# Differential attention on one core: TensorE's value products placed ahead of the transposes within a step

## What is computed

```python
def attend_block(args):                      # diff_attention, one block of 128 queries
    logits = jnp.einsum('bhmqd,bhmkd->bhmqk', qb, k).astype(jnp.float32)
    logits = logits + jnp.transpose(bias, (2, 0, 1))[None, :, None]
    logits = jnp.where(visible, logits, -jnp.inf)
    p = jax.nn.softmax(logits, axis=-1)
    w = p[:, :, 0] - lam * p[:, :, 1]
    return jnp.einsum('bhqk,bhkv->bhqv', w.astype(v.dtype), v)
...
o = rms_norm(o, out_norm_g) * (1.0 - lam_init)

# memory_cross_attention
logits = jnp.einsum('bqhd,bkhd->bhqk', q, k).astype(jnp.float32)
p = jax.nn.softmax(logits, axis=-1)
o = jnp.einsum('bhqk,bkhd->bqhd', p.astype(v.dtype), v)
```

## Time and profile before

| what | value |
|---|---|
| median of 3 runs | 3560.15 us (3557.86 to 3570.12) |
| the profiled execution | 3560.86 us, its span 3559.1 us |
| TensorE busy | 3274.8 us (92%), granted clock 0.955 in the mean |
| VectorE busy | 2348.2 us (66%) |
| ScalarE busy | 974.5 us (27%) |
| GpSimd busy | 1077.6 us (30%) |
| the stage of the change | 2304.4 to 2393.0 us of the span, about 88 us |

### The profile page before, as it was taken

The page is one execution under the profiler, slowest core; times in us unless marked ns, Lnnn a source line. Parts: engine busy times, 40 slices in busy tenths (PEclk is TensorE's granted clock), DMA queues, the critical chain, the costliest instruction groups (busy, mean ns, idle before and its releaser), DMA issues. The chain is left out here.

```text
span 3559.1 us, 53901 instructions
## 1 busy us (share of the span) xinstructions
PE 3274.8 (92%) x18869; PEld 2888.2 (81%) x18869; DVE 2348.2 (66%) x4071; ACT 974.5 (27%) x1683; POOL 1077.6 (30%) x751
## 2 busy tenths in 40 slices
PE   8769999697999999998999998979998998799989
PEld 6458898475999999998999997747886767578867
DVE  5565565746888988877888887476774324367741
ACT  2222222202333343333333333361210012311200
POOL 4111010341121222213333333304554432045544
PEclk9879999898999999999999999999999998699999
DMA  4000000222778777788999992103332320033323
GB/s 139 32 1 2 1 1 1 73 68 96 240 250 272 248 264 258 246 293 319 359 353 340 348 338 91 51 16 99 99 103 65 92 72 14 15 98 94 97 71 97
DMA packets 214325, 508.78 MB, mean 143 GB/s; under 512 B 18534, under 2 KB 102646, under 8 KB 210588
## 3 DMA queue, kind: packets, MB, share of 16 engines
q1 hardware_dynamic: 155420, 322.15, 27.1%
q0 software_dynamic: 36864, 134.23, 11.5%
q10 hardware_dynamic: 21888, 50.34, 3.7%
HBM read 454.21 MB, written 52.44 MB: 142 GB/s over the span
## 5 line engine op out<-in xcount | busy, mean ns | idle before, releaser
L177 PE MATMUL ev_acc<-ev_w_high,ev_high 128*128 128x384 f32 x1024 | 343.1, 335 | 9.2 <-DVE ev_w_low L2365 9.2
L178 PE MATMUL ev_acc<-ev_w_low,ev_high 128*128 128x384 f32 x1024 | 342.8, 335 | 0.0
L179 PE MATMUL ev_acc<-ev_w_high,ev_low 128*128 128x384 f32 x1024 | 342.8, 335 | 0.0
L177 PE MATMUL up_ps<-ffn_high,up_high 128*128 128x512 f32 x704 | 276.0, 392 | 5.5 <-DVEq L646 5.5
L2315 POOL DMA_INDIRECT ev_rows<-in_v,ev_list x128 | 177.4, 1386 | 333.5 <-DVE ev_row_sum L2370 322.8
L179 PE MATMUL up_ps<-ffn_high,up_low 128*128 128x512 f32 x704 | 275.4, 391 | 0.0
L178 PE MATMUL up_ps<-ffn_low,up_high 128*128 128x512 f32 x704 | 275.1, 391 | 0.0
L177 PE MATMUL eu_ps<-norm_unit_high,eu_high 128*128 128x384 f32 x768 | 265.1, 345 | 0.0
L172 POOL TENSOR_TENSOR up_low<-normed,up_high 128x1024 fp32r<-128x1024 f32 x88 | 211.4, 2403 | 176.7 <-DVE up_high L167 176.7
L179 PE MATMUL eu_ps<-norm_unit_high,eu_low 128*128 128x384 f32 x768 | 257.2, 335 | 0.0
L178 PE MATMUL eu_ps<-norm_unit_low,eu_high 128*128 128x384 f32 x768 | 257.0, 335 | 0.0
(11 more groups left out here) (602 smaller groups left out, 8377.8 us busy)
## 6 DMA issues: line engine op xcount, KB each, us to landing
normed<-in_u SPq DMA_DIRECT2D x128, 512.0 KB, 4.8
mixed<-in_v SPq DMA_DIRECT2D x128, 512.0 KB, 5.4
normed<-in_w_up SPq DMA_DIRECT2D x88, 512.0 KB, 3.5
expert_act<-mixed ACTq DMA_DIRECT2D x128, 192.0 KB, 4.2
expert_gates<-eu_gates ACTq DMA_DIRECT2D x24, 1024.0 KB, 6.9
expert_scores<-expert_gates SPq DMA_DIRECT2D x16, 1536.0 KB, 10.9
ev_act<-expert_act SPq DMA_DIRECT2D x128, 192.0 KB, 5.6
in_w_raw<-in_w_in SPq DMA_DIRECT2D x20, 512.0 KB, 3.5
```

What stands on the lines that cost most here:

```text
L177: nc.tensor.matmul(out, w_high.bitcast(F32R), x_high.bitcast(F32R), start=start, stop=False)
L178: nc.tensor.matmul(out, w_high.bitcast(F32R), x_low.bitcast(F32R), start=False, stop=False)
L179: return nc.tensor.matmul(out, w_low.bitcast(F32R), x_high.bitcast(F32R), start=False, stop=stop)
```

## The change

Two things in `diff_attention` move; no instruction is added or taken away. On TensorE `add_values(s - 3)` now stands ahead of `turn(s - 2)`. On ScalarE `take_memory` now stands ahead of `keep(s - 2)`; without that TensorE would wait in step 31 for a copy that stands in ScalarE's queue behind a `keep` which waits for TensorE's own later transposes. `square` stays behind `keep`.

```diff
@@ -2535,10 +2535,10 @@
                 for s in range(steps):
                     if s < n_items:
                         score(s)
+                    if 0 <= s - 3 < n_items:
+                        add_values(s - 3)
                     if 0 <= s - 2 < n_items:
                         turn(s - 2)
-                    if 0 <= s - 3 < n_items:
-                        add_values(s - 3)
                     if diff_behind(s, 5) is not None:
                         length(diff_behind(s, 5))
 
@@ -2638,11 +2638,13 @@
                     if s < n_items:
                         raise_(s, 0)
                         raise_(s, 1)
+                    h = head_behind(s, 4)
+                    if h is not None and h >= DH:
+                        take_memory(h - DH)
                     if 0 <= s - 2 < n_items:
                         keep(s - 2)
-                    h = head_behind(s, 4)
-                    if h is not None:
-                        square(h) if h < DH else take_memory(h - DH)
+                    if diff_behind(s, 4) is not None:
+                        square(h)
                     if diff_behind(s, 5) is not None:
                         root(diff_behind(s, 5))
```

## The result

| | before | changed |
|---|---|---|
| median of the runs | 3560.38 us (6 runs, 3557.86 to 3570.12) | 3586.53 us (6 runs, 3585.13 to 3588.30) |
| ratio | | 1.0057, 95% interval 1.0043 to 1.0071 |
| the profiled execution | 3560.86 us, span 3559.1 | 3585.41 us, span 3583.7 |

The change makes the kernel 26 us slower. I had forecast 7. Forecast and result have the same sign, and the result lies outside the range of 3556 to 3574 us. To a loss of more than 10.7 us I had given a chance of 0.18.

A forecast was written before the change was run, and what follows sets the result against it. The attention stage was taken as a loop of waits, a head's period running through TensorE's queue and VectorE's `take_out`; 0.1 + 2.6 + 0.8 + 1.0 - 0.5 + 3.0 = +7.0 us on 3560.15 gave 3567 us, range 3556 to 3574.

The forecast's parts named there:

- The order's terms: Attention stage: delays from exposed transposes, late copies and lost cover, less the gain from `take_memory` first; sum +7.0 us.
- first head: First head of the attention stage: value products gain nothing in waits for weights, block-3 products meet their copy; 0.1 us lost.
- four rounds: Four of five rounds between heads: each 0.65 us longer by exposed transposes, late copies and lost cover; 2.6 us.
- fifth round: Round into the memory items: the same 0.31 us, plus cover of four transposes falling away; 0.8 us together.
- memory items, `take_memory`, end: Stage's last part: exposed transposes and missed copies +1.0 us, `take_memory` first -0.5, transposes, copy and products running uncovered +3.0.
- the exposed transposes: Block 1's two transposes leave the wait for `take_out` and stand behind the first product; 0.31 us a head.
- the lost cover: Block 3's products come directly behind the scores and wait for ScalarE's copy, formerly covered by a transpose; 0.24 us.
- the round's term: A head's round: 0.31 us for transposes, 0.1 for block 1's products, 0.24 for block 3's; 0.65 us in sum.
- the part on the clock: TensorE's low clock stretches, in three of five rounds, cost about 1.4 us each; a longer unbroken wait could bring more.
- its rival: The clock falls in more rounds: three more low stretches at 1.4 us, 4.2 us added, 3571 us; chance 0.17.
- the signs of being wrong: Full-clock round of 10.33 us or less, stage's end still near 4.8 us, or low clock stretches changing in number.
- What bounds the kernel now: Prediction's opening part: attention stage is a loop of waits, cut off by barriers, so its length change alone enters the time.

The follow-up runs named there:

- Filled against filled: Change and kernel before, each with two matmuls of no use per wait for `take_out`: 3565.66 and 3566.23 us, attention stage 90.2 and 84.1 us.
- the wait of 2.54 us alone: Kernel before with products ahead of transposes only in the steps where TensorE waits for `take_out`, ScalarE as in the change: 3573.77 us, ratio 1.0030.
- the other half of the change alone: Kernel before with products ahead of transposes in steps up to 30 except those waiting for `take_out`, ScalarE as in the change: 3574.32 us, ratio 1.0032.
- the shifted runs: Kernel before with five VectorE copies of no use starting gated linear attention: 3571.65 us, ratio 1.0020; the change with six: 3587.01 us, ratio 1.0057.
- both fillings: Matmuls of no use in waits for `take_out` and in gated linear attention's early TensorE waits: kernel before 3559.58 us, change 3563.77 us.
- the early `take_out`: VectorE's `take_out` put before `bias(s, 0)`: kernel before 3564.67 us, change 3566.71 us; kernel before with work of no use in both stages' waits 3556.88 us.

## Why the prediction was wrong

**The order's terms held.** Filled against filled, from start to start:

| term | forecast | measured |
|---|---|---|
| first head | 0.1 | 0.1 (15.5 against 15.4 us to the first `take_out`) |
| four rounds | 2.6 | 2.0 (10.76 against 10.27) |
| fifth round | 0.8 | 0.65 (9.99 against 9.34) |
| memory items, `take_memory`, end | 1.0 - 0.5 + 3.0 = 3.5 | 3.4 (21.0 against 17.7) |
| sum | 7.0 | 6.1 |

The last of these terms can be read without fillings too, since both kernels are at full clock there: 20.9 against 17.2 us, 3.6. The wait for `take_out`, the exposed transposes and the lost cover are where I put them. In the first head the waits in front of transposes fell from 3.0 to 1.3 us, but the head didn't get shorter, so the value products gained nothing there either. Only the round's term was too large, 0.65 us where it is 0.49. In the two filled timelines above, the first product to the next scores is 0.63 us (2341.78 to 2342.41) instead of 0.42 (2343.77 to 2344.19), so the exposed transposes cost 0.21 and not 0.31. The block-2 scores to block 3's products take 1.04 us (2346.72 to 2347.76), of which 0.19 is the wait that I had at 0.24; but from the block-2 to the block-3 scores it is only 2.24 us (to 2348.96) instead of 2.17 (2348.29 to 2350.46). The lost cover thus costs 0.07 net, because products and transposes in their new places take 0.12 less. The other 0.21 of the round lie between, in block 1's products and behind them, where I had 0.1.

**The clock's term was mis-sized.** The sum has nothing for it. In the part on the clock and in its rival I took the low stretches at 1.4 us each and three more at worst, 4.2 us, at a chance of 0.17. They came in all five rounds, two more than before, and three of them lasted twice as long. The first two rounds, 12.26 and 12.31 us against 10.76 filled, pay 1.5 us each; the last three, 13.46 and 13.55 against 10.76 and 12.79 against 9.99, pay 2.7 to 2.8. The part is 11.1 us instead of 4.3, +6.8: about 3 for the two more, the rest for the longer ones. I had counted stretches at the price they had before and had no term for their length. Nor did that price follow from its working: 11.04 against 10.33 over five rounds and three stretches gives 1.2, since the fifth round, 9.40 without a low stretch, is shorter for another reason. Against full-clock rounds of 10.33 the measured 11.89, 11.75 and 11.89 give 1.4 to 1.6. The rival that the part on the clock calls the third is the first in the list, the clock's. That the low stretches change in number is one of the signs of being wrong that I had named. The reason I gave, the longer unbroken wait, doesn't hold by itself: with the wait of 2.54 us alone, or with the other half of the change alone and a wait of 2.17, four rounds had one. What makes the stretches longer stays open.

**The step that failed outright** is the sentence in "What bounds the kernel now": *what the stage gains or loses in length goes into the time one for one, and nothing else moves*. The barriers do cut the stages off from each other in data and queues, but not in the clock. Gated linear attention takes 93.0 or 101.8 us by the course of the clock in it, and the shifted runs show that this course hangs on the start; by the two groups of its runs the kernel before has the short course in more than half of them, and the change in none of its six (all lie within 3.2 us of each other at a mean clock of 0.947 or 0.948, and the profiled one has the long course). This is +8.8 us that no row of the changed stage could give. The two groups were in sight in the numbers: the runs shown, 3557.86, 3560.15 and 3570.12, lie 12.3 us apart, and I took that as plain scatter.

**The sum**: 6.1 by order, 6.8 by clock in the stage, 8.8 by clock in the later stage make 21.7 of 26.2 us. The remaining 4 or so stay open; the profile has 3.9 before the stage, in unchanged code, where all profiles scatter (the stage starts between 2304.0 and 2311.4), and no run tells whether the change has a part in it. The medians put more on the clock than these two profiles do: both fillings take 22.8 us off the change (3586.53 to 3563.77) and 1.2 off the kernel before (3560.79 to 3559.58), and 4.2 us are left for the order.

## What to carry to other kernels

Before moving work out of a wait, ask what the wait covers: here it hid the transposes, and placed behind it they went into the one chain that sets the round. A stage with repeated TensorE waits, such as the 2.2 to 2.5 us here, can have several lengths, by the clock; compare two orders with the waits filled by work of no use, and only then read the order's own price. Look for the wait's cause before reordering around it: moving VectorE's copy earlier in its step shortened the full-clock round by 0.8 us.

## What the runs showed of the hardware

- The same 344 matmuls of a stage took 93.0 or 101.8 us of stage time by the clock alone (0.63 against 0.50 in the mean), and a shift of its work by 2.3 us turned a mixture of the two into times and clocks of the long one in all 12 runs.
- Behind waits of 2.17 to 2.54 us the clock fell in one to five of five rounds, with the same instructions in one and in three of them. Each low stretch lasted about 3.4 or 6.8 us and cost 1.4 to 1.6 or 2.7 to 2.8. With 1.9 us of matmuls or 1.75 us of float32 transposes in each wait the clock stayed at 1.00 through all five rounds, in each of the five profiles.
- Work of no use made a kernel faster: the change fell from 3586.53 to 3563.77 us by it. The fastest version, which also has the early `take_out`, does 56 transposes and 6 matmuls whose results nobody reads.
